# A selection threshold found bit by bit from sums of signs, in place of rounds of eight maxima

## The reference

```python
sc = indexer_scores(qib, iwb, ki)                       # 128 queries x 1024 keys, sum over 8 heads of w * relu(q.k)
sc = jnp.where(key_pos[None, None, :] <= q_pos[None, :, None], sc, -jnp.inf)
_, sel = lax.top_k(sc, topk)                            # topk = 256
valid = sel <= q_pos[None, :, None]
ks = gather_rows(k, sel)
vs = gather_rows(v, sel)
logits = jnp.einsum('bthd,btkhd->bthk', qb, ks, preferred_element_type=jnp.float32) * ATTN_SCALE
p = jax.nn.softmax(jnp.where(valid[:, :, None, :], logits, -jnp.inf), axis=-1)
```

## Time and profile before

| | |
|---|---|
| time, median of 3 runs (lowest, highest) | 2133.17 us (2128.34, 2134.04) |
| the profiled execution's own time, its span | 2133.78 us, 2132.0 us |
| TensorE matmul | 1947.4 us busy, 91% |
| VectorE | 976.4 us, 46% |
| ScalarE | 639.8 us, 30% |
| GpSimd | 519.4 us, 24% |
| MAX8 (L1727), MATCH_REPLACE8 (L1731) | 201 each, 175.1 and 171.8 us |
| mean granted clock of TensorE | 0.913 |

### The profile page before, as it was taken

How to read it: one execution, slowest core, us unless ns; L and a number is a source line. 1 busy time by engine, 2 the same in 40 slices (tenths; PEclk the granted TensorE clock), 3 DMA queues, 4 the chain that set the end, 5 groups by cost and what they waited for, 6 DMA issues and landing times.

```text
span 2132.0 us, 30147 instructions
## 1 busy us (share of the span) xinstructions
PE 1947.4 (91%) x12564; PEld 1155.7 (54%) x12667; DVE 976.4 (46%) x1649; ACT 639.8 (30%) x1315; POOL 519.4 (24%) x416
## 2 busy tenths in 40 slices
PE   6899999896887678999979999999999999899999
PEld 3523444343563355454448864444444444489998
DVE  4855999999758778335522212421222222300000
ACT  5442223444203476133223321322222222201000
POOL 1100456576001310011000030024233332332200
PEclk9855999997658789999989989999999999999999
DMA  6010112102332210210023330211112123022211
GB/s 189 16 44 1 45 55 89 53 16 90 110 116 73 90 41 2 95 40 1 30 70 105 103 119 40 84 40 57 43 40 60 40 60 94 18 83 87 89 36 29
DMA packets 132306, 132.72 MB, mean 62 GB/s; under 512 B 15294, under 2 KB 105150, under 8 KB 132132
## 3 DMA queue, kind: packets, MB, share of 16 engines
q1 hardware_dynamic: 130506, 126.33, 18.5%
q0 software_dynamic: 1664, 4.46, 0.7%
HBM read 114.78 MB, written 15.98 MB: 61 GB/s over the span
## 4 chain that ended last, share of the span: by engine, by line
PE 56%; ACT 1%; DVE 1%; issue 0%; DMA 0%; ACTq 0%
PE PS L1216 8%; PE PS L1214 8%; PE PS L1215 7%; PE PS L760 5%; PE PS L761 4%; PE PS L762 4%; PE PS L1234 4%; PE PS L1235 4%; PE PS L1236 4%; PE PS L1133 1%; PE PS L1152 1%; PE PS L1089 1%; PE PS L1090 1%; PE PS L1110 1%; ACT arena L1250 1%; PE PS L1111 1%
## 5 line engine op out<-in xcount | busy, mean ns | idle before, releaser
L760 PE MATMUL PS<-arena 128*128 128x512 f16 (+3 forms) x856 | 312.7, 372 | 24.7 <-POOL arena L321 14.1
L761 PE MATMUL PS<-arena 128*128 128x512 f16 (+3 forms) x856 | 311.9, 371 | 0.0
L1216 PE MATMUL PS<-arena 128*128 128x512 f16 (+1 forms) x1056 | 298.4, 318 | 2.5 <-issue 0.2
L1250 ACT ACTIVATE arena<-PS 128x512 f32<-128x512 f32 (+13 forms) x365 | 176.3, 510 | 413.7 <-PE PS L762 126.0
L1214 PE MATMUL PS<-arena 128*128 128x512 f16 (+1 forms) x1056 | 298.7, 318 | 0.0
L762 PE MATMUL PS<-arena 128*128 128x512 bf16 (+2 forms) x809 | 292.7, 369 | 0.0
L1215 PE MATMUL PS<-arena 128*128 128x512 bf16 (+1 forms) x1012 | 286.3, 315 | 0.0
L321 POOL TENSOR_TENSOR arena<-arena 128x2048 bf16<-128x2048 f32 (+2 forms) x38 | 140.5, 3720 | 494.0 <-ACT arena L314 493.9
L1234 PE MATMUL PS<-arena 128*128 128x256 f16 (+1 forms) x792 | 217.1, 274 | 5.8 <-DVE arena L746 5.8
L1235 PE MATMUL PS<-arena 128*128 128x256 f16 (+1 forms) x792 | 217.0, 274 | 0.0
L1236 PE MATMUL PS<-arena 128*128 128x256 bf16 (+1 forms) x792 | 216.9, 274 | 0.0
(11 more groups left out here) (221 smaller groups left out, 3149.7 us busy)
## 6 DMA issues: line engine op xcount, KB each, us to landing
arena<-w_gu SPq DMA_DIRECT2D x44, 512.0 KB, 3.9
arena<-w_down SPq DMA_DIRECT2D x8, 1408.0 KB
arena<-w_in SPq DMA_DIRECT2D x8, 1024.0 KB, 5.5
arena<-x_prompt SPq DMA_DIRECT2D x16, 512.0 KB, 7.6
arena<-w_kv_mem SPq DMA_DIRECT2D x8, 1024.0 KB, 6.8
arena<-cache_mem_k SPq DMA_DIRECT2D x32, 256.0 KB, 2.6
arena<-cache_mem_v SPq DMA_DIRECT2D x32, 256.0 KB, 3.2
arena<-w_in SPq DMA_DIRECT2D x24, 256.0 KB, 3.6
```

Source lines behind the costliest of these rows:

```text
L760: e.matmul(out, x_hi(k)[:, cols], wh[:, q, :], start=(q == 0), stop=False)
L761: e.matmul(out, x_lo(k)[:, cols], wh[:, q, :], start=False, stop=False)
L1216: mm = e.matmul(out, wl, xa_hi[:, k, t0:t0 + tn], start=False, stop=(k == KT - 1))
L1250: e.activation(out, in_, ACT.Copy, **kw).then_inc(sem(name), 1)
```

## The change

Blocks 2, 3 and 4 keep their rounds (96 of them). For blocks 5, 6 and 7 (RADIX, 768, 896 and 1024 columns) the 256th largest score of each query is found bit by bit. ScalarE takes the sign of score minus candidate over each block and adds the signs up (`sign_step`: three ACTIVATEs with a sum, scale and bias from pointers, output int8 that nobody reads). VectorE compares the sums with a goal and sets the next bit of the candidate (`radix_step`). There are 32 such steps. The first 25 stand in L4 (after the parts g = 0 and 2 of the chunks t = 0 and 1, and after each value tile), the other 7 in the sampled tokens' attention. VectorE runs an update and then 4 rounds (conv) or 2 rounds (value) of blocks 2 to 4 at each step, and the remaining 14 one for each item of the Q and K projections. At the end `selection` turns each candidate into the mask: it counts what lies above its two bounds, picks the value, ranks ties by a scan, and writes the mask, in three turns a block after one common turn. These ten turns stand in the memory part. The core of the diff:

```diff
-ROUNDS_BEFORE, ROUNDS_ITEM, ROUNDS_SAMPLE0, ROUNDS_SAMPLE, ROUNDS_TOKENS, ROUNDS_KEYS, ROUNDS_MEMORY, \
-    ROUNDS_VALUES, ROUNDS_ATT = \
-    116, (1, 2), 7, 3, 1, 3, 1, 13, 1
+RADIX = (5, 6, 7)
+NR = len(RADIX)
+BITS = 32
+ROUNDS_CONV, ROUNDS_VALUE, ROUNDS_ITEM, ROUNDS_SAMPLE, ROUNDS_TOKENS, ROUNDS_KEYS, ROUNDS_MEMORY, \
+    ROUNDS_VALUES, ROUNDS_ATT = 4, 2, 1, 1, 1, 2, 3, 3, 1
...
+        def has_step(x):
+            return L4[x][0] == "v" or (L4[x][2] < 2 and L4[x][3] != 1)
...
+            def sign_step():
+
+                if steps[0] == BITS:
+                    return
+                e.wait_ge(sem("rx_cand"), steps[0] + 1)
+                for a, i in enumerate(RADIX):
+                    n = (i + 1) * P
+                    kw = dict(bias=rx_cand[:, a:a + 1], scale=rx_sign[:, a:a + 1]) if steps[0] else {}
+                    x = e.activation(rx_junk[a][:, 0:n], work[:, topk_cols(i):topk_cols(i) + n], ACT.Sign,
+                                     accum_out=rx_sum[:, a:a + 1], **kw)
+                x.then_inc(sem("rx_sum"), 1)
+                steps[0] += 1
+
             for x, item in enumerate(L4):
+                if x >= 1 and has_step(x - 1):
+                    sign_step()
...
+            sign_step()
+            e.wait_ge(sem("rx_sum"), steps[0])
             e.wait_ge(sem("conv_lo"), NC_T)
             project_items(NI1, NI)
...
+                if b == 0:
+                    e.wait_ge(sem("st_out"), 32)
+                sign_step()
...
+            def radix_step(k):
...
+                bit = BITS - 1 - k
+                if k >= 1:
+                    flip = (1 << bit) | (1 << bit - 1 if bit else 0)
+                    link(e.tensor_scalar(rx_base[:, :], rx_cand_i[:, :], flip, None, ALU.bitwise_xor))
+                e.wait_ge(sem("rx_sum"), k + 1)
...
+                link(e.tensor_tensor(rx_bit[:, :], rx_sum[:, :], rx_goal[:, :], ALU.is_ge))
+                e.scalar_tensor_tensor(rx_cand_i[:, :], rx_bit[:, :], bit, rx_base[:, :], ALU.logical_shift_left,
+                                       ALU.bitwise_or).then_inc(sem("rx_cand"), 1)
+                e.wait_ge(sem("rx_cand"), k + 2)
...
+                for a, i in enumerate(RADIX):
+                    n = (i + 1) * P
+                    x = work[:, topk_cols(i):topk_cols(i) + n]
+                    one = slice(a, a + 1)
+
+                    for v, over in ((rx_low, rx_over_low), (rx_high, rx_over_high)):
+                        link(e.tensor_scalar(tie[:, 0:n], x, v[:, one], None, ALU.is_gt, ALU.add,
+                                             accum_out=over[:, one]))
...
+                    link(e.tensor_scalar(tie[:, 0:n], x, rx_v[:, one], None, ALU.is_equal))
+                    link(e.tensor_tensor_scan(tie_rank[:, 0:n], tie[:, 0:n], tie[:, 0:n], 0.0, ALU.add, ALU.max))
+                    yield
+
+                    link(e.scalar_tensor_tensor(tie[:, 0:n], tie_rank[:, 0:n], rx_rest[:, one], tie[:, 0:n], ALU.is_le,
+                                                ALU.mult))
+                    link(e.scalar_tensor_tensor(tie[:, 0:n], x, rx_v[:, one], tie[:, 0:n], ALU.is_gt, ALU.add))
+                    done[0] += TOPK // 8
+                    e.tensor_scalar(x, tie[:, 0:n], -MASKED, MASKED, ALU.mult, ALU.add).then_inc(sem("topk"), 1)
...
-            turn(ROUNDS_BEFORE)
+            for x in range(len(L4)):
+                if has_step(x):
+                    update()
+                    turn(ROUNDS_VALUE if L4[x][0] == "v" else ROUNDS_CONV)
             for L in range(NI1, NI + 2):
...
-                if L < NI:
-                    turn(ROUNDS_ITEM[L % 2])
-
-
-            turn(ROUNDS_SAMPLE0)
+                if L < NI and done[0] < 3 * TOPK // 8:
+                    turn(ROUNDS_ITEM)
+
+
             for b in range(DEC_B):
+                if b >= 1:
+                    update()
```

More of the change, by code:

```diff
@@ L11 @@
 I32 = mybir.dt.int32
+I8 = mybir.dt.int8
 ALU = mybir.AluOpType
@@ L44 @@
 NEG = -3.0e38
+TINY = 2.0 ** -126
 MASKED = -1.0e30
@@ L452, in build @@
         N4C = NC_T * 9
+        def has_step(x):
+            return L4[x][0] == "v" or (L4[x][2] < 2 and L4[x][3] != 1)
+        STEPS_L4 = len([x for x in range(len(L4)) if has_step(x)])
         ATT = [(i, hh) for i in range(NB) for hh in range(H)]
@@ L480, in build, with radix_state @@
         N3 = Norm("n3", tiles, lambda j: h[0:rows(j), j, :], xa_hi, xa_lo, None)
+        junk = view("KI", 2048, [D], BF16)
         NM = Norm("nm", [P, P], lambda j: memx[:, j, :], xm_hi, xm_lo,
-                  lambda e, j: e.wait_ge(sem("memx_ld"), 32), junk=view("KI", 1024, [D], BF16), gain=g_src)
+                  lambda e, j: e.wait_ge(sem("memx_ld"), 32), junk=junk, gain=g_src)
+        def radix_state(k, dt=F32, n=NR):
+            return view("KI", 4112 + 16 * k, [n], dt)
+        rx_sum, rx_goal, rx_pos, rx_sign, rx_cand = (radix_state(k) for k in range(5))
+        rx_cand_i, rx_base, rx_bit, rx_pos_i, rx_neg_i = (radix_state(k, I32) for k in (4, 5, 6, 7, 2))
+        rx_low, rx_high, rx_tmp, rx_over_low, rx_over_high, rx_v, rx_rest = (radix_state(8 + k) for k in range(7))
+        rx_low_i, rx_high_i = radix_state(8, I32), radix_state(9, I32)
+        rx_junk = [view("KI", shift, [(i + 1) * P], I8) for i, shift in zip(RADIX, (2496, 576, 1472))]
+        tie = view("SP", 0, [SEQ], F16)
+        tie_rank = view("SP", 2 * SEQ, [SEQ], F16)
         xnorm = view("QI", 0, [2, D])
@@ L1739, in _ @@
             marked(work_s[:, :])
+            for a, i in enumerate(RADIX):
+                x = e.memset(rx_goal[:, a:a + 1], float(2 * TOPK - 1 - (i + 1) * P))
+            x.then_inc(sem("rx_cand"), 1)
+            def radix_step(k):
[4 more added lines that the diff above has]
+                e.wait_ge(sem("rx_sum"), k + 1)
+                if k == 0:
+                    link(e.tensor_tensor(rx_pos[:, :], rx_sum[:, :], rx_goal[:, :], ALU.is_ge))
+                    link(e.tensor_scalar(rx_sign[:, :], rx_pos[:, :], 2.0, -1.0, ALU.mult, ALU.add))
+                    link(e.tensor_scalar(rx_tmp[:, :], rx_goal[:, :], 2.0, -1.0, ALU.mult, ALU.add))
+                    link(e.tensor_tensor(rx_tmp[:, :], rx_tmp[:, :], rx_pos[:, :], ALU.mult))
+                    link(e.tensor_scalar(rx_goal[:, :], rx_goal[:, :], -1.0, 1.0, ALU.mult, ALU.add))
+                    link(e.tensor_tensor(rx_goal[:, :], rx_goal[:, :], rx_tmp[:, :], ALU.add))
+                    e.memset(rx_cand[:, :], -2.0).then_inc(sem("rx_cand"), 1)
+                    e.wait_ge(sem("rx_cand"), 2)
+                    return
+                link(e.tensor_tensor(rx_bit[:, :], rx_sum[:, :], rx_goal[:, :], ALU.is_ge))
+                e.scalar_tensor_tensor(rx_cand_i[:, :], rx_bit[:, :], bit, rx_base[:, :], ALU.logical_shift_left,
+                                       ALU.bitwise_or).then_inc(sem("rx_cand"), 1)
+                e.wait_ge(sem("rx_cand"), k + 2)
             def selection():
-                for i in range(2, NB):
+                for i in range(2, RADIX[0]):
                     v = work[:, topk_cols(i):topk_cols(i) + (i + 1) * P]
@@ L1757, in turn, with update @@
                     next(rounds, None)
-            turn(ROUNDS_BEFORE)
+            updates = [0]
+            def update():
+                if updates[0] < BITS:
+                    radix_step(updates[0])
+                    updates[0] += 1
+            for x in range(len(L4)):
+                if has_step(x):
+                    update()
+                    turn(ROUNDS_VALUE if L4[x][0] == "v" else ROUNDS_CONV)
             for L in range(NI1, NI + 2):
@@ L1778, in _ @@
                                 ).then_inc(sem("sa_p"), 1)
-                turn(ROUNDS_SAMPLE)
+                if done[0] < 3 * TOPK // 8:
+                    turn(ROUNDS_SAMPLE)
+            while updates[0] < BITS:
+                update()
             e.wait_ge(sem("sa_hi"), 1)
@@ L1810, in _ @@
                     if i >= 2 and hh == 0:
-                        turn(max(0, TOPK // 8 * (i - 1) - taken[0]))
+                        while done[0] < TOPK // 8 * (i - 1):
+                            turn(1)
                         e.wait_ge(sem("topk"), i)
```

31 lines of the change are left out of this document (28 added, 3 removed).

## The result

| | before | after |
|---|---|---|
| time, median (lowest, highest) | 2130.76 us (2125.38, 2134.04) | 2188.08 us (2184.99, 2192.67) |
| runs | 4 | 4 |
| ratio, 95% interval | | 1.0273 (1.0243 to 1.0304) |
| span of the profiled execution | 2132.0 us | 2183.2 us |

A forecast was written before the change was run, and what follows sets the result against it. TensorE, busy 91% of the span, was taken as the bound. Terms 41.7 - 8 + 2.5 + 5 = +41 on the median of 2133.17 gave 2174 us, range 2150 to 2192, the forecast's own range 2164 to 2186.

The forecast's parts named there:

- rival B: Slow handshake: each update 1.0 us or more and steps of 3.6; L4 +50, time 2184; chance 0.08.
- L4, +41.7: Conv and value projections: sign steps and waits for VectorE's updates delay the last eviction to 427.9; +41.7 us (+36 to +52).
- The step of 3.3 us: ScalarE's sign step, three ACTIVATEs with a sum over 768, 896 and 1024 columns: 3.3 us (3.0 to 3.6).
- the update: VectorE after each sum: two operations on 128x3 and a semaphore, with gaps 0.4 us (0.2 to 1.0).
- Q and K projections, -8: Q and K projections: TensorE's long rotary wait goes as VectorE arrives with nothing owed; -8 us (-4 to -11).
- The 7.26: TensorE's longest wait for GpSimd's rotary in the Q and K projections, behind the 116 rounds; 7.26 us, to go.
- Sample loop, +2.5: Sampled tokens: first Exp gains 1.63 us, signs of 3.3 stand before key copies in early blocks; +2.5 us (0 to +5).
- rival C: Sign not in Exp's table: two loads of 1.28 us around each sample-loop sign; time 2184; chance 0.07.
- Memory keys, +5 (+2 to +8): Memory keys: three finishing turns replace one round before the second head norm, sum of squares 5 us late; +5 us.
- the 10.71: TensorE's 10.71 us wait at 701.78 in the memory keys, behind GpSimd's weight split; expected still about 10.
- A (rounds don't pace): L4: rounds don't pace the sign steps, the conv tile's 38.4 us chain alone decides; L4 +30, time 2162; chance 0.12.
- D: L4: signs hidden in ScalarE's idle time, L4 ends as before, key stage unharmed; time 2124; chance 0.05.

The follow-up runs named there:

- Experiment 9: Kernel before with 112 instead of 116 rounds ahead of the Q and K projections, the other four at the end of the memory part: 2133.47 us, ratio 1.0010.
- Experiments 1: Changed kernel with no finishing turns ahead of the second memory head norm, all behind the last head norm: 2171.47 us, ratio to before 1.0192.
- experiment 2: Changed kernel with three finishing turns kept ahead of the second head norm, the later ones all behind the last: 2180.20 us, ratio 1.0227.
- experiment 4: Changed kernel with 2 rounds instead of 4 behind each conv update, the 32 left over in the sample loop: 2170.25 us, ratio 1.0181.
- experiment 8: Changed kernel, conv signs in ScalarE's idle times, finishing turns late, three value-part signs moved to the sample loop; also called the best version: 2126.88 us, ratio 0.9974.
- experiment 3: Changed kernel with each sign ACTIVATE reading only the first 64 columns, goals scaled down, steps and waits kept: 2163.68 us, ratio 1.0145.

## Why the prediction held, step by step

Forecast 2174 (2150 to 2192), measured 2188, the sign right. It is 2 us above the own range of the forecast, 2164 to 2186. In the profiled pair the terms come to +51.2 where they were forecast at +41.2: L4 is 5.6 over and the memory keys 6.7 over, and the Q and K projections (1.3) and the sample loop (1.0) give back a little. One sum of the range was wrong: the ends of the four terms add up to +27 and +61, which is 2160 to 2194, and by its +50 for L4 rival B is 2182 and not 2184. The measured time lies inside 2160 to 2194 too. By term:

**L4, +41.7, measured +47.0 to +47.3.** The mechanism is the one predicted and the dates lie close: first evictions 259.27, 300.78 and 344.44 for 260.0, 300.3 and 342.8; the ends of the signs of the second tile 265.9, 271.1, 276.7 and 282.3 for 265.9, 270.2, 275.2 and 280.8; the waits 3.8, 1.6 and 9.2 for 2.9, 2.3 and 9.4. The step of 3.3 us was 3.35 (groups of ScalarE by shape: count, busy us, mean ns of one):

```profile
L1356 ACT ACTIVATE arena<-arena 128x1024 int8<-128x1024 f32 x32 | 39.2, 1226 | 0.0
L1356 ACT ACTIVATE arena<-arena 128x896 int8<-128x896 f32 x32 | 35.8, 1120 | 0.0
L1356 ACT ACTIVATE arena<-arena 128x768 int8<-128x768 f32 x32 | 32.6, 1019 | 19.9 <-DVE arena L1810 19.9
```

What was mis-sized is the update, "with gaps 0.4 us (0.2 to 1.0)". Alone it is 0.35 (272.93 to 273.28). At the first update after a weight split it is far more, here at the first value tile (VectorE, then GpSimd):

```profile
396.19 2.95 DVE L1809 TENSOR_TENSOR arena<-arena 128x3 int32<-128x3 f32 x1 [11.83 <-ACT arena L1356]
399.17 1.08 DVE L1810 SCALAR_TENSOR_TENSOR arena<-arena 128x3 int32<-128x3 int32 x1
```
```profile
391.02 8.10 POOL L325 TENSOR_TENSOR arena<-arena 128x2048 bf16<-128x2048 f32 x2 [0.53 <-ACT arena L318]
399.08 1.15 POOL L2130 TENSOR_TENSOR arena<-gb,arena 128x512 bf16<-128x512 f32 x1
```

An operation on three columns took 2.95 us and ended at 399.14, when GpSimd's split ended at 399.12. The same at 266.06 (1.43), 307.57 (1.44) and 352.09 (2.93): with the 1.08 some 9 us more than alone. I left it out of the sum. In the conv part the missing time comes in where it strikes: the three conv tiles with such an update last 1.2, 1.2 and 2.1 us longer than forecast, so that the fourth tile's first eviction is 1.6 us late and the first value tile is evicted at 388.08 for 384.3. At the first value tile it cost nothing: behind that step ScalarE was idle for 2.82 us ahead of the third value tile. That one is evicted at 406.56 for 401.2, and the 1.6 us more are the split's end (11.0 us behind the first value tile's eviction, for 10.3) and what follows it (7.4, for 6.6).

**Q and K projections, -8, measured -9.3.** The 7.26 went, as predicted; of the waits for the rotary 11.5 us in 4 are left, where 21.1 in 7 stood. Experiment 9 takes four rounds from in front of this wait and gives 7.3. The line from 433 to 551:

```profile
PE PS L806 <- POOL arena L2155: 11.5, 4, 5.0
```

**Sample loop, +2.5, measured +1.5.** A table load at each sign (rival C) would have shown here; from 551 to 681 there is one load, as before:

```profile
L1419 ACT ACT_TABLE_LOAD x1 | 1.3, 1283 | 0.0
```

**Memory keys, +5 (+2 to +8), measured +11.7.** The place was right, the size was not, and it is the term outside its bounds. I had read one wait on this chain, the 10.71 of the earlier trace rows, and expected it to stay at about 10. There are two, and the turns fell mainly on the other, which was 3.41 before:

```profile
677.98 0.39 PE L760 MATMUL PS<-arena 128*128 128x512 f16 x1 [3.41 <-POOL arena L321]
```

It became 10.91, and the 10.71 became 13.98. Experiments 1 and 2 divide it: the turns ahead of the second norm cost 9.6 us against none at all (7.8 against the kernel before, which had one round there; I had 5), the turns behind it 3.9, which were in no term. I had looked only at the slot before the sum of squares, and not at what the next slot falls upon (TensorE's waits of the stage; VectorE; GpSimd):

```profile
725.14 0.61 PE L783 MATMUL PS<-arena 128*128 128x512 f16 x1 [10.91 <-POOL arena L325]
752.99 0.61 PE L783 MATMUL PS<-arena 128*128 128x512 f16 x1 [13.98 <-POOL arena L325]
```
```profile
715.16 1.14 DVE L1862 SCALAR_TENSOR_TENSOR arena<-arena 128x896 f16<-128x896 f16 x1
716.34 4.83 DVE L1864 SCALAR_TENSOR_TENSOR arena<-arena 128x896 f16<-128x896 f32 x1
721.21 4.36 DVE L1866 TENSOR_SCALAR arena<-arena 128x896 f32<-128x896 f16 x1
```
```profile
715.47 9.61 POOL L325 TENSOR_TENSOR arena<-arena 128x2048 bf16<-128x2048 f32 x2 [82.76 <-ACT arena L318]
```

Two operations that take 1.15 and 0.63 us in experiment 2 took 9.2 together beside GpSimd's split, and the third norm stood behind them. The scan over 896 columns took 2.02 us, within the bounds of one and two passes.

**The rivals.** A (rounds don't pace) falls by experiment 4 and by the waits for L1810. B's price was nearly met (2184) by another mechanism, which is chance: the update is cheap by itself and dear beside GpSimd. C falls by the row above. D is refuted for this order of the work, but not for the work: experiment 8 hides the 20 steps that it has in L4 (+0.3 us), pays 4.9 over the kernel before for the 12 in the sample loop, and comes to 2126.9, where D had said 2124. That "ScalarE idles too little at the right places" was a property mainly of where the steps stood.

## What to carry to other kernels

Cost new work by the gap that it falls into, not by the engine's idle share: 25 steps behind the evictions cost L4 47 us, 20 steps put mostly in ScalarE's waits for GpSimd cost it 0.3, and the other five cost the sample loop 3.4. In an exchange of two engines the distance between steps is set by whatever stands ahead of the short answer on the other engine; halving the rounds ahead of the update gave as much (13.9 us) as cutting a step from 3.35 us to 1.3 (14.0). And when engine work is removed, first measure what the critical engine ever waited for it: here 7.3 us by experiment 9, and 10.8 for the whole Q and K stage in the best version, of 151.

## What the runs showed of the hardware

Operations of VectorE with two inputs in SBUF, and some with one, didn't run while a TENSOR_TENSOR of GpSimd ran. On three columns they ended within 0.02 us of its end: 0.16 us became 1.43 to 2.95. The two over 896 columns ended 0.95 and 0.48 us behind the end of one of its two instructions: 1.15 became 4.83, 0.63 became 4.36. GpSimd was held too: its pair of splits went from 8.10 to 9.61. MAX8 and MATCH_REPLACE8, with one input each, kept their times beside it (0.56 and 0.54 over 384 columns at 289.54 and 290.21, during GpSimd's sum of 289.48 to 292.00 in the changed kernel). In experiment 3 the update's second operation started at 261.12, took 3.02 and ended at 264.14; GpSimd's split ended at 264.12:

```profile
261.12 3.02 DVE L1811 SCALAR_TENSOR_TENSOR arena<-arena 128x3 int32<-128x3 int32 x1
```
```profile
257.96 6.16 POOL L325 TENSOR_TENSOR arena<-arena 128x1536 bf16<-128x1536 f32 x2 [2.08 <-ACT arena L318]
```

The Trainium skill (SBUF — State Buffer, Who interferes with whom) states this: an instruction of VectorE with two SBUF inputs contends with a GpSimd instruction that reads SBUF, the later one is blocked until the other ends, and one with a single input outside the two-port modes isn't. The trace agrees in the rows with two inputs and in those of MAX8 and MATCH_REPLACE8. For the TENSOR_SCALAR, with one input, it agrees only if that ran in a two-port mode, which no run here shows. All this was read from the rows only; no run took GpSimd's work away. A TENSOR_TENSOR_SCAN cost 2.2 ns a column (2.29 us over 1024, 2.02 over 896), 1.8 times a SCALAR_TENSOR_TENSOR (1.28 over 1024).
